# Four fifths of a first mixer moved between the gather rows, and half of the rows laid out as two experts for 64 tokens

## The reference, cut to what matters

```python
# x: 512 tokens of 1024, ahead of them 16 meta tokens (h has 528 rows)
hn = rms_norm(h, g_mix)
xv, bg, cg, ga, gg = split(hn @ w_in)                 # five parts of 512 channels
y_sc = bg * causal_depthwise_conv(cg * xv, w3)        # 3 taps
y_cf = silu(layer_norm(causal_depthwise_conv(ga * sigmoid(gg), w31) + b))   # 31 taps
h = h + concat(rms_norm(y_sc), rms_norm(y_cf)) @ w_out
hn = rms_norm(h, g_ffn)
# PEER: 8 heads, two key halves of 128, top 16 of 16 x 16 candidates
idx, gates = peer_route(hn @ w_q, sub_keys)           # [token, head, 16]
act = gelu(einsum("chkd,cd->chk", u[idx], hn))
h = h + einsum("chk,chkd->cd", act * gates, v[idx])
x = rms_norm(h, g_final)[:, 16:]
# then a second block on x: half FFN, attention (two kinds of heads), half FFN
```

## Time and profile before

| what | value |
|---|---|
| median of 3 runs | 2440.91 us (2438.84 to 2445.41) |
| span of the profiled execution | 2440.3 us |
| busy PE / DVE / ACT / POOL | 2117.7 / 1829.9 / 1180.3 / 751.1 us |
| bytes moved | 760.89 MB, 536.90 of them by the gathers |

### The profile page before, as it was taken

One profiled execution on the slowest core, in us unless ns is written; L12 is line 12 of the kernel. 1 busy time (PEld: TensorE's weight loads), 2 busy tenths in 40 slices (PEclk: granted clock), 3 DMA queues, 4 the chain that ended last, 5 costly groups with the idle time before them and its releaser, 6 DMA issues. The chain is left out here.

```text
span 2440.3 us, 28668 instructions
## 1 busy us (share of the span) xinstructions
PE 2117.7 (87%) x9528; PEld 1505.2 (62%) x9528; DVE 1829.9 (75%) x3369; ACT 1180.3 (48%) x3781; POOL 751.1 (31%) x634
## 2 busy tenths in 40 slices
PE   6987898897777776999784688699989999999999
PEld 6966444343222223885343467388539988898997
DVE  6985686777988888989889988866675656656664
ACT  5213556555666665343455555433344446445443
POOL 0000445445554554233456544433320001100000
PEclk9988899999999998999896679799999999999999
DMA  5211999999999999999999999999986444224454
GB/s 200 86 52 52 377 417 414 422 404 421 419 421 421 416 420 369 390 405 420 417 402 368 377 406 420 416 403 420 421 343 207 177 175 161 75 99 156 177 187 138
DMA packets 107460, 760.89 MB, mean 312 GB/s; under 512 B 12064, under 2 KB 12832, under 8 KB 16432
## 3 DMA queue, kind: packets, MB, share of 16 engines
q0 software_dynamic: 73728, 536.90, 53.9%
q1 hardware_dynamic: 33584, 222.15, 23.9%
HBM read 756.91 MB, written 2.10 MB: 311 GB/s over the span
## 5 line engine op out<-in xcount | busy, mean ns | idle before, releaser
L2448 POOL DMA_INDIRECT pair<-in_uv,idx x512 | 639.6, 1249 | 850.3 <-DVE resid L1079 519.5
L1837 ACT ACTIVATE smalls<-smalls 128x1 f32<-128x1 f32 (+1 forms) x2058 | 540.1, 286 | 640.5 <-DVE smalls L1747 622.3
L1747 DVE CUSTOM_DVE_ANT_0 pair<-pair,hn 128x1024 f32<-128x1024 f32 x512 | 624.2, 1221 | 179.8 <-DMA pair<-in_uv,idx 178.4
L596 PE MATMUL bank<-pair,diag 128*128 128x512 f32 x928 | 452.3, 619 | 124.5 <-ACT diag L1837 124.3
L596 PEld LDWEIGHTS bank<-pair,diag 128*128 128x128 f32 x928 | 167.3, 192 | 389.9 <-ACT diag L1837 243.9
L596 PE MATMUL bank<-ft,raw 128*128 128x256 f32 x1664 | 375.4, 389 | 11.9 <-DVE ft L1073 11.9
L596 PEld LDWEIGHTS bank<-ft,raw 128*128 128x128 f32 x1664 | 324.6, 196 | 58.7 <-issue 12.7
L1079 DVE SCALAR_TENSOR_TENSOR resid<-pair,smalls,resid 128x1024 f32<-128x1024 f32 x275 | 352.4, 1281 | 0.6 <-ACT smalls L1837 0.6
L1073 DVE TENSOR_TENSOR half<-raw,half 128x1024 fp32r<-128x1024 f32 (+1 forms) x204 | 235.6, 1194 | 124.6 <-ACT half L1837 123.2
L1837 ACT ACTIVATE half<-raw 128x1024 fp32r<-128x1024 f32 (+1 forms) x204 | 199.5, 1026 | 128.9 <-PE bank L596 128.8
L596 PE MATMUL bank<-ft_hi,half 128*128 128x256 f32 x960 | 178.4, 287 | 1.5 <-DVE ft_early L1073 1.5
(11 more groups left out here) (288 smaller groups left out, 2966.2 us busy)
## 6 DMA issues: line engine op xcount, KB each, us to landing
raw<-in_wts SPq DMA_DIRECT2D x196, 1024.0 KB
pair<-in_uv,idx POOLq DMA_INDIRECT x512
raw<-in_wts SPq DMA_DIRECT2D x10, 512.0 KB
raw<-in_wts SPq DMA_DIRECT2D x4, 720.0 KB
resid<-in_x SPq DMA_DIRECT2D x4, 512.0 KB, 6.3
out<-resid SPq DMA_DIRECT2D x8, 256.0 KB, 5.7
raw<-in_wts SPq DMA_DIRECT2D x2, 768.0 KB
rowt<-in_rows SPq DMA_DIRECT2D x1, 1076.0 KB, 12.6
```

The costliest lines, as they stand in the source:

```text
L596: return e.matmul(o, a, b, start=start, stop=stop)
L1747: e.tensor_tensor_reduce(b[:, 0:1024], b[:, 0:1024], HN[i // 128], 1.0, 0.0, ALU.mult, ALU.add, actv[:, i % 8:i % 8 + 1]).then_inc(dotted, 1)
L1837: return e.activation(o, i, f, **kw)
L2448: e.indirect_dma_start(pair[i % NPAIR], None, uv, bass.IndirectOffsetOnAxis(ap=idx[:, n % SLOTS, k:k + 1], axis=0)).then_inc(pairs_in[i % ...
```

## The change

Tile 0 and the 16 meta tokens (`TILE0_TOKENS` = 144) go through the mixer first, with plain f32 products (`tile0_in`, ten pieces of 16 products of 128x144) from weights that SP loads straight into the seven pair buffers and the three raw ones (`FIRST_LOADS`). As soon as head 0 of tile 0 has its route, the gathers begin. The other 384 tokens' mixer is spread between rows: 20 pieces `rest_in` (eight products of 128x384) at the rows of `PIECE_ROW`, tile 0's heads 3 to 7 at those of `Q_ROW`, the sums, the layer norm (`MEAN`, `VAR`) and the output products up to row 103, then scores of tiles 1 to 3 in nine calls at `CALL_ROW`. DVE does the taps for the 384 tokens between dots, two a row. `sc`, `bg` and `wout` are read again for it through the ring, and `wr` now covers eight heads.

The first 256 rows (`HALF`, tiles 0 and 1) hold two experts for 64 tokens each: `hn` is doubled over the partitions (`doubled`, HD), the lists of indices and gates are brought into that order by small products and copies (`permute` on PE, `lists_back` on DVE), `diag` has 64 columns, and `add_pair` adds two rows with four products whose outputs lie in either half of a bank's partitions. All of these rows are on PE. The gathers 4 to 7 go to buffers in which the `cf` weights for the rest still lie, and wait for the pieces that read them.

```diff
-ORDER = ([(("cf", i), 2048) for i in range(4)] + [(("sc", i), 2048) for i in range(4)]
-         + [(("bg", i), 2048) for i in range(2)] + [(("wout", i), 2048) for i in (0, 2, 1, 3)]
-         + [(("wq", i), 2048) for i in range(8)] + [(("wr", i), 2048) for i in range(2)] + chain_order("A") + chain_order("B"))
+TILE0_TOKENS, REST = 144, 384
+FIRST_LOADS = ([(("cf", i), "pair", 3 + i) for i in range(4)] + [(("sc", i), "pair", i) for i in range(3)]
+               + [(("sc", 3), "raw", 0), (("bg", 0), "raw", 1), (("bg", 1), "raw", 2)]
+               + [(("wout", 0), "pair", 0), (("wout", 2), "pair", 1), (("wout", 1), "pair", 2), (("wout", 3), "raw", 0)])
+ORDER = ([(k, 2048) for k in [("wq", 1), ("wq", 2), ("sc", 0), ("sc", 1), ("wq", 3), ("sc", 2), ("sc", 3), ("bg", 0), ("wq", 4),
+                              ("bg", 1), ("wq", 5), ("wout", 0), ("wout", 2), ("wq", 6), ("wq", 7), ("wout", 1), ("wout", 3)]]
+         + [(("wr", i), 2048) for i in range(8)] + chain_order("A") + chain_order("B"))
...
-ON_PE = [i < HALF + 8 and not (i < 128 and i % 4 == 3) or LAST_ON_PE <= i < PAIRS - 2 for i in range(PAIRS)]
+ON_PE = [i < HALF + 8 or LAST_ON_PE <= i < PAIRS - 2 for i in range(PAIRS)]
...
+PIECE_ROW = [0, 0, 0, 0, 0, 1, 2, 3, 8, 11, 14, 16, 22, 25, 28, 31, 34, 37, 42, 45]
+Q_ROW = {3: 19, 4: 39, 5: 48, 6: 69, 7: 74}
+SC_SQUARES, SC_OUT = 56, [57, 59, 61, 63, 65, 67]
+MEAN, VAR = 80, 84
+CALLS = [(0, 1, 2), (1, 1, NT), (2, 1, NT), (0, 2, NT)] + [(h, 1, NT) for h in range(3, 8)]
+CALL_ROW = [104, 118, 124, 129, 136, 142, 150, 158, 166]
...
+            def rest_in(n):
+
+                name, c, j = PIECES[n]
+                if name == "cf":
+                    e.wait_ge(slots_in[3 + c], 16)
+                    w = pair[3 + c].rearrange("p (k n) -> p k n", k=8)
+                else:
+                    w = ring_weights((name, c), 8)
+                o, done = fresh("R", n)
+                for kt in range(8):
+                    ins = mm(o[:, 0:REST], w[:, kt, j * P:(j + 1) * P], XTR[:, kt, :], kt == 0, kt == 7)
+                ins.then_inc(done, 1)
...
+            def add_pair(i):
+
+                t = i // 128
+                e.wait_ge(diagd, i + 2)
+                for h in range(2):
+                    if i % 128 == 0:
+                        fresh("mix", 2 * t + h)
+                    b = B["mix", 2 * t + h]
+                    for j in range(2):
+                        ins = mm(bank[b.bank][64 * j:64 * j + 64, :], diag[(i + j) % 8][:, 0:64],
+                                 pair[(i + j) % NPAIR][:, 1024 + h * 512:1536 + h * 512], i % 128 == 0, i % 128 == 126)
+                ins.then_inc(v_used, 1)
...
+                if i < 2:
+                    filled(e, "ysc", i)
+                elif i == 2:
+                    filled(e, "ycf", 0)
+                elif i < NPAIR:
+                    filled(e, "R", 2 * (i - 3) + 1)
+                else:
+                    row_used(e, i - NPAIR)
```

More of the change, by code:

```diff
@@ L90 @@
         SPLITS.append(W[_key])
-EARLY = sum(c.key[0] in SPLIT_NAMES for c in SPLITS)
+EARLY = 0
 NPAIR = 7
@@ L429, in program @@
         tact, wgt, minus = small(8), small(8), small(1)
-        pair = [ar(f"pair{i}", PAIR + 2048 * i, 2048) for i in range(NPAIR)]
         LAYER = CHAIN + 6144
@@ L571, in loads @@
                 e.dma_start(dst[:], src).then_inc(late_in, 16)
+            e.dma_start(wq0, wts[CHUNKS["wq"][0]]).then_inc(wq0_in, 16)
+            e.dma_start(kbuf, wts[CHUNKS["keys"][0]]).then_inc(keys_in, 16)
+            for n in range(10, 14):
+                first(n)
             def store(p):
@@ new lines, in vector, with weave @@
+            e.memset(warm, 1.0).then_inc(padded, 1)
+            e.wait_ge(const_in, 32)
+            tt(id2, idt[:, 0:64], idt[:, 64:128], ALU.add).then_inc(masks, 1)
+            mean_of(0, 0, 16)
+            mean_of(0, 1)
+            tile_in(0, 16, 0)
+            tile_in(1, P, 16)
+            mean_of(0, 2)
+            T = TILE0_TOKENS
+            taps0 = [conv(YT0[:, 4 + ct, :], upad0, "cf", 31, ct, 16, P, ct + 1, taps_done) for ct in range(4)]
+            def weave(n, a, b_=None):
+                while n:
+                    before = n
+                    for g in (a, b_):
+                        if g is not None and n and next(taps0[g], 0) is None:
+                            n -= 1
+                    if n == before:
+                        return
@@ new lines, in vector, with pump, rest_u @@
+            taps = [conv(YTR[:, 4 + ct, :], upadr, "cf", 31, ct, 0, REST, 9 + ct, taps_done) for ct in range(4)]
+            def pump(n):
+                while n and taps:
+                    if next(taps[0], taps) is taps:
+                        taps.pop(0)
+                    else:
+                        n -= 1
+            def rest_u(ct):
+                o, out_ = filled(e, "R", 2 * ct)
+                taken(e, "R", 2 * ct + 1)
+                tt(upadr[:, ct, 30:30 + REST], o[:, 0:REST], tmpr[ct % 2], ALU.mult).then_inc(out_, 1)
@@ L1776, in vector @@
                 pass
-            for t in (2, 3):
-                y_added(t)
-            for t in (2, 3):
-                mean_of("hn", t)
-            for t in (2, 3):
-                row_out(t)
-            first, steps = Paced(chain("A")), iter(())
+            lists_back(0)
+            first, steps, between = Paced(chain("A")), iter(()), Paced(rest())
             for n in range(32):
@@ L2435, in gates, with rest @@
                 e.tensor_scalar(gat[:, r, :], gat[:, r, :], sm[:, r, 2:3], 0.5, ALU.mult, ALU.mult).then_inc(gated, 1)
+            def rest():
+                yield 64
+                y_rate("ms", 1, 1, 4)
+                for stage, t, due in (("m", 1, 98), ("m", 2, 101), ("s", 1, 103), ("s", 2, 107), ("m", 3, 110), ("s", 3, 115)):
+                    yield due
+                    if stage == "m":
+                        y_rate("mc", t, 4 + t, 5 + t)
+                    else:
+                        rate("hn", t)
             e.wait_ge(padded, 4)
-            for h in range(2):
-                filled(e, "y_cf", 6 + h)
-            first = Paced(chain("A"))
+            gates(0)
+            first, between = Paced(chain("A")), Paced(rest())
             for i in range(PAIRS):
```

1163 lines of the change are left out of this document (719 added, 444 removed).

## The result

The changed kernel takes 2451.89 us (median of 20 runs, 2445.55 to 2459.41), the kernel before 2443.55 in the same comparison: a ratio of 1.004 [1.003, 1.0051]. It is 0.4% slower, where 0.8% faster was forecast. The ratio is that of the fast runs; one of the 20 of the kernel before took 2770.35 us and is left out of it. The profiled execution has a span of 2455.4 us, 15.1 more than before. It took 2457.3 us, 5.4 above the median, so about a third of the 15.1 belongs to this one execution.

The account below looks back on a forecast made before the run. The end is set by the first gather's start, the bytes until the last gather and an unchanged tail. 2440.3 - 92 (start) + 40 (bytes) + 32 (work no longer hidden) gave 2420 us, main case 2390 to 2440, whole range 2370 to 2465.

Parts of the forecast that it names:

- First gather, 138; gather 16 near 196: Start of the gathers: first leaves at 138 us, 105 earlier; the 16th near 196, 92 earlier than 288.26.
- The price of a pair, 2.2: PE's addition of two rows in rows 0 to 175: 2.2 us, between bounds of 1.94 and 3.87.
- Rival A: Pairs on PE: the halves run one after the other, PE binds rows 0 to 175, time 2520 us; chance 0.17.
- rival D: PE drains at each change between 64 and 128 columns, some 13 us in rows 0 to 175, time 2433; chance 0.06.
- "Nothing hides this", +40 for bytes: Between gathers 16 and 176, 23 weight chunks follow instead of 7: 16 x 2.52 = +40 us, DMA engines being the bound.
- "What no longer hides", +24: Mixer work between rows 16 and 175: largest of DMA, DVE and PE sums per 16 rows, 483 against 459 for DMA.
- row 87, +8: At row 87 PE waits for ACT's silu output, seven buffers covering it: about three rows of transfers, +8 us.
- Gathers 176 to 256 "in 202 us as now": Rows after the mixer's work: gathers 176 to 256 take 202 us, unchanged.
- Rival B: Rows 16 to 175: no overflow, pairs being cheap and blocks lending slack through seven buffers; time 2388 us; chance 0.18.
- Rival C: First rows: round trips through banks that ACT and DVE empty, three waits at pieces 4 to 9 cost 24; 2445 us; chance 0.13.
- Gathers 256 to 512 and the tail: The rest of the kernel: 898.2 us for these gathers and 633 us from the last gather to the end, unchanged.

Follow-up runs that it names:

- run 6: The changed kernel with a pair's four products reordered, both halves of the sum for one row, then for the other: 2450.06 us, ratio 1.0037.
- Run 9: The changed kernel with both rows of every pair but a tile's first added into the same half of the partitions: 2528.54 us, ratio 1.0339.
- run 10: The changed kernel with 18 weight chunks of the ring loading an eighth of their bytes, all instructions kept: 2444.28 us, ratio 1.0006.
- run 5: The changed kernel with eight score calls cut into quarters two rows apart, with banks of their own and one weight chunk read once more: 2424.36 us, ratio 0.9921.
- run 3: The changed kernel with rows 176 to 255 added one by one, each freeing its buffer alone: 2446.11 us, ratio 1.001.
- runs 8: The changed kernel with quartered calls, single rows from 176, gates on DVE, the mixer's output products spread and tile 0's head 2 at row 6: 2412.44 us.
- 12: The kernel of run 8 with pieces 8 to 19 of the mixer's input products cut into halves two rows apart: 2410.58 us, ratio 0.9866.
- 16: The kernel of run 8 with ACT's block of silu, squares and gains spread over three rows: 2410.8 us, ratio 0.9869.
- run 2: The changed kernel with eight score calls cut into halves, the first half two rows earlier: 2456.45 us, ratio 1.0051.

## Why the prediction was wrong, point by point

- **First gather, 138; gather 16 near 196.** Right in kind, too late by 22 and 20 us. The term that was mis-sized is the pass of tile 0's pieces: 0.117 to 0.172 us, not 0.181, and with it their end is at 58 us, not 76. Gathers 6 and 7 wait 11.45 and 11.18 us for pieces, at the place named.
- **The price of a pair, 2.2.** Measured 1.8 back to back and 1.94 alone, with its end: the lower bound. The Trainium skill, TensorEngine Tiling (Array Packing), Key Properties, lets different tiles multiply in parallel; the trace agrees (1.8 in two halves, 3.5 in one). The forecast's reason for 2.2, that only neighbours of different halves can overlap, is false too: run 6 takes 3.70 for two pairs whose products follow each other half by half. Rival A is false in its premise. Run 9 shows its price for a pair to be near (3.5, not 3.87), but that its 2528.54 lies near A's 2520 is luck: A put 100 us on a forecast of 2420, and the run is 76.7 above a kernel of 2451.89. Of rival D, the drain at a change of tiling mode that the same section states, nothing shows that could be priced: the pair at 562.88 starts where the call with 128 columns ends, and takes 1.94.
- **"Nothing hides this", +40 for bytes.** The bytes are there, 777.73 MB against 760.89, which is the 16 chunks. But run 10 takes 39.7 us of them away and gets 7.6 back. They travel in gaps that the waits leave, so they may not be added to a term for those waits.
- **"What no longer hides", +24, and row 87, +8. This is the step that failed.** It took the larger of three sums for each 16 rows, as if engines with in-order queues overlapped fully and seven buffers bridged the rest. Together with the bytes it gave 490.4 us for gathers 16 to 176; they took 539.7, with pairs that were cheaper than assumed. Of the 49 us, 20 lie in gathers 128 to 176 (168.6 against 149 forecast), and run 5 gives back 31 there by cutting blocks of up to 11.8 us into four: shown, by the time and by the gaps in the queue of the gathers. Some 30 lie in gathers 16 to 128, 19 of them in 80 to 112 (112.6 against 94 with the wait at row 87); what causes them is open for the most part. The layer norm's steps account for 5 to 7 there, and in 16 to 80 the work of PE and DVE is only a likely cause. At row 87 the forecast saw one wait; the trace shows several.
- **Gathers 176 to 256 "in 202 us as now".** They took 213.4. Two rows are released at once, which had no term; run 3 shows it, at some 7 us in the mean of the executions and 11 in this one.
- **Rival B** (no overflow) is false. **Rival C** had waits in a round, which is right in kind, but the wrong ones: it put them at banks that ACT and DVE empty and ahead of gather 16, which left before 196. Those that showed hold the rows' buffers, behind PE's calls and in the layer norm, most of them from gather 80 on. So that the measured time lies near C's 2445, and inside the range that C stretched to 2465, is luck.
- **Gathers 256 to 512 and the tail** are as before, so the reading of the rest of the kernel holds.

What the change sought can be had from its early start: with calls cut up, rows released singly and the mixer's end spread, runs 8, 12 and 16 take 2411 to 2412 us, 1.3% under the kernel before and 1.6% under the change.

## What to carry to other kernels

Before comparing sums of work, compare the longest block of an in-order engine with the transfers that are under way when the block begins. Here seven of eight calls of 8.8 to 11.8 us left the queue of the gathers empty, quarters of 2.85 us did not, and halving blocks of 5.4 us gave nothing that shows. A term for more bytes and a term for waits may not simply be added: here most of the bytes lay in gaps that the waits left. When no engine is full in a stretch, look for who holds a buffer, cut that block, and keep a bank and a loaded weight ready for the pieces, or a new wait takes its place (run 2).

## What the runs showed of the hardware

- Two f32 products with 64 columns of weights for different halves of the partitions run together in both orders that were tried (3.65 and 3.70 us for two pairs); for the same half they take turns (7.08).
- PE's pairs that follow a wait can take 3.3 to 3.7 us in place of 1.9, at the lower of its two clock levels (the pair at 431.28 takes 3.68 at a granted clock of 0.50); the change has 18 of those between gathers 16 and 176, 17 of them behind a wait of 1.3 to 7.4 us. Products put into the waits raise the granted clock from 0.83 and 0.87 to 0.97 and make the kernel no faster (2410.8 us without, 2419.24 with two behind each pair).
